# RWKV-7 recurrence in chunks: level 0 of the triangular inverse taken from the left sides by copies and 32x32 transposes

## The reference, cut to what matters

```python
def step(S, inp):
    r_t, w_t, k_t, v_t, kk_t, a_t = inp
    sa = jnp.einsum('bhvk,bhk->bhv', S, kk_t)
    S = S * w_t[:, :, None, :] - sa[..., None] * (kk_t * a_t)[:, :, None, :] + v_t[..., None] * k_t[:, :, None, :]
    y = jnp.einsum('bhvk,bhk->bhv', S, r_t)
    return S, y
S, ys = lax.scan(step, S0, xs)
```

## Time and profile before

| what | value |
|---|---|
| median of 3 runs | 1197.93 us (1197.78 to 1203.37) |
| the profiled execution | span 1197.4 us; the page gives no other time of it |
| four units of the recurrence | 411 to 611 us |
| their successor: last steps, output projection, routing, experts | 611 to 1197 us |
| TensorE busy | 1120.7 us (94%) |
| VectorE, ScalarE, GpSimd busy | 464.6, 363.2, 259.6 us |
| mean granted TensorE clock | 0.980 |

### The profile page before, as it was taken

How to read it: one execution, slowest core, us unless ns; L and a number is a source line. 1 busy time by engine, 2 the same in 40 slices (tenths; PEclk the granted TensorE clock), 3 DMA queues, 4 the chain that set the end, 5 groups by cost and what they waited for, 6 DMA issues and landing times.

```text
span 1197.4 us, 24875 instructions
## 1 busy us (share of the span) xinstructions
PE 1120.7 (94%) x10856; PEld 785.9 (66%) x10856; DVE 464.6 (39%) x930; ACT 363.2 (30%) x808; POOL 259.6 (22%) x153
## 2 busy tenths in 40 slices
PE   5999999999999988788889999889999999999995
PEld 4666666655566667667654444478778887888774
DVE  4200657447765586675835422441101000111034
ACT  3101545444334365563621311111111111011152
POOL 0000000001110179999800000111112112111102
PEclk9999999999999999999999999889999999999998
DMA  6511100010010210002051661268889989998894
GB/s 207 153 36 36 57 18 19 18 31 27 25 37 18 35 37 4 5 4 56 7 182 36 236 226 71 93 221 306 268 310 323 312 290 319 322 322 295 299 387 170
DMA packets 95689, 174.16 MB, mean 145 GB/s; under 512 B 19988, under 2 KB 41175, under 8 KB 95172
## 3 DMA queue, kind: packets, MB, share of 16 engines
q1 hardware_dynamic: 88372, 151.92, 36.6%
q0 software_dynamic: 7200, 20.57, 6.4%
HBM read 147.45 MB, written 27.75 MB: 146 GB/s over the span
## 4 chain that ended last, share of the span: by engine, by line
PE 85%; DVE 8%; ACT 3%; issue 3%; SPq 0%; DMA 0%; POOLq 0%; POOL 0%; DVEq 0%; ACTq 0%
PE ps L740 23%; PE ps L1446 20%; PE ps L1244 9%; PE ps L1469 9%; PE ps L1475 1%; PE ps L819 1%; PE ps L843 1%; PE ps L832 1%; PE ps L1422 1%; PE ps L956 1%; PE ps L944 1%; PE ps L997 1%; PE ps L1099 1%; PE ps L1122 1%; PE ps L1309 1%
## 5 line engine op out<-in xcount | busy, mean ns | idle before, releaser
L740 PE MATMUL ps<-arena 128*128 128x355 f32 x960 | 299.3, 468 | 2.2 <-issue 2.1
L1446 PEld LDWEIGHTS ps<-arena 128*128 128x128 f32 x2048 | 245.9, 191 | 7.8 <-issue 6.1
L740 PEld LDWEIGHTS ps<-arena 128*128 128x128 f32 x960 | 180.2, 191 | 107.6 <-issue 10.4
L1446 PE MATMUL ps<-arena 128*128 128x128 f32 (+4 forms) x2048 | 248.3, 283 | 0.7 <-ACT arena L1958 0.6
L1244 PE MATMUL ps<-arena 128*128 128x512 f32 x256 | 116.6, 597 | 0.9 <-DVE arena L2346 0.7
L1469 PE MATMUL ps<-arena 128*128 128x512 f32 x256 | 113.3, 595 | 0.7 <-DVE arena L2621 0.7
L1966 ACT ACTIVATE arena<-ps 128x128 f32<-128x128 f32 (+4 forms) x64 | 18.3, 286 | 278.5 <-PE ps L1446 278.5
L2621 DVE TENSOR_TENSOR arena<-arena,ps 128x128 f32<-128x128 f32 (+4 forms) x64 | 19.1, 299 | 212.7 <-ACT arena L1966 212.7
L1469 PEld LDWEIGHTS ps<-arena 128*128 128x128 f32 x256 | 47.4, 190 | 55.1 <-issue 53.6
L2806 POOL TENSOR_TENSOR arena<-arena 128x1024 f32<-128x1024 f32 x4 | 11.4, 2858 | 330.5 <-DVE arena L2147 330.5
L1555 ACT COPY arena<-ps 128x355 f32<-128x355 f32 x60 | 27.2, 453 | 183.1 <-PE ps L740 183.1
(11 more groups left out here) (416 smaller groups left out, 1567.4 us busy)
## 6 DMA issues: line engine op xcount, KB each, us to landing
arena<-in_w_exp_gate SPq DMA_DIRECT2D x16, 2048.0 KB
arena<-in_w_exp_up SPq DMA_DIRECT2D x16, 2048.0 KB
arena<-in_w_exp_down SPq DMA_DIRECT2D x16, 2048.0 KB, 15.4
arena<-in_w_in SPq DMA_DIRECT2D x16, 512.0 KB, 3.8
arena<-in_x_prompt SPq DMA_DIRECT2D x9, 512.0 KB, 4.5
x_dram<-arena SPq DMA_DIRECT2D x9, 512.0 KB, 3.6
h_dram<-arena SPq DMA_DIRECT2D x8, 512.0 KB, 2.6
out_y_prompt<-arena SPq DMA_DIRECT2D x8, 512.0 KB, 3.5
```

The costliest lines, as they stand in the source:

```text
L740: last = pe.matmul(ps[:, q % 2, 0:m], wr[:, n % 3, k, :], hT[:, k, a:a + m], start=(k == 0), stop=(k == KB - 1))
L1446: last = pe.matmul(ps[:, 3 + f % 2, n * CAP:n * CAP + CAPS[e]], w[a][:, k, f * P:(f + 1) * P], xgT[:, a, k, 0:CAPS[e]], start=(k == 0), st ...
```

## The change

Level 0 is no longer computed by products of its own. The identities go into U (not TL); a predicated copy puts the level-0 entries of the raw left side (B side, from PSUM) into U, under the transposed level mask. ScalarE copies U to TT (64 partitions at a time where rows are exchanged), VectorE turns U by 32x32 blocks into TL. ScalarE, not VectorE, copies the B side out, both banks in one copy and without a mask. The mask of its second half follows at the end of the unit (`r_reaching`), and `r_ra` waits for it. TensorE's order becomes `r_left` 0, 1, `r_u(0, 1)`, `r_gain` 0, `r_u(1, 1)`, `early_fill`, `r_gain` 1, `step`, `r_x(0, 1)`.

```diff
@@ TensorE
-            def r_cross(hp, b):                 (its 32 products per unit go)
             def r_gain(hp, b):
-                pe.wait_ge(s["rl_ok"], 4 * m + 4)
+                pe.wait_ge(s["rl_ok"], 4 * hp + b + 3)
             def r_u(hp, b, lv):
                 if lv == 1:
-                    pe.wait_ge(s["rc_ok"], m + 1)
+                    pe.wait_ge(s["rl_act"], m + 1)
+                    pe.wait_ge(s["tr_own"], nth(hp, b, 1, LV - 1))
             def r_ra(hp, b):
                 pe.wait_ge(s["rm_ok"], 2 * m + 2)
+                pe.wait_ge(s["lm_ok"], m + 1)
-                r_cross(hp, 0)
-                r_gain(hp, 0)
                 for lv in range(1, LV):
                     r_u(hp, 0, lv)
                     if lv == 1:
-                        r_cross(hp, 1)
+                        r_gain(hp, 0)
+                        r_u(hp, 1, lv)
+                        early_fill(hp, lv)
                         r_gain(hp, 1)
-                        early_fill(hp, lv)
-                        r_u(hp, 1, lv)
                         step(hp, c)
@@ ScalarE
+            def left_raw(hp, b):
+                act.wait_ge(s["rl_ok"], 4 * hp + b + 1)
+                act.copy(LB[:, b].rearrange("p u j c -> p u (j c)"), ps[:, 4 * b:4 * b + 2, :]).then_inc(s["rl_act"], 1)
+            def first_turned(hp, b):
+                act.wait_ge(s["rl_ok"], 4 * hp + b + 1)
+                flat = lambda ap: ap.rearrange("p j t -> p (j t)")
+                for e in range(2):
+                    act.copy(flat(TT[row(e), b, JB:2 * JB, :]), flat(U[row(1 - e), b, JB:2 * JB, :]))
+                act.copy(flat(TT[:, b, 0:JB, :]), flat(U[:, b, 0:JB, :])).then_inc(s["tr_ok"], 1)
             def u_out(hp, b, lv):
+                if lv == 1:
+                    act.wait_ge(s["tr_ok"], nth(hp, b, 1, LV - 1))
-                    act.copy(TL[:, b], T["eye64"]...).then_inc(s["r_eye"], 1)
+                    act.copy(U[:, b], T["eye64"]...).then_inc(s["r_eye"], 1)
-                gained(hp, 0)
+                left_raw(hp, 0)
+                first_turned(hp, 0)
+                left_raw(hp, 1)
                 for lv in range(1, LV):
-                    swap_rows(hp, 0, lv - 1)
+                    if lv > 1:
+                        swap_rows(hp, 0, lv - 1)
                     u_out(hp, 0, lv)
+                    if lv == 1:
+                        first_turned(hp, 1)
+                        gained(hp, 0)
                     first_fill(hp, lv)
+                    if lv > 1:
+                        swap_rows(hp, 1, lv - 1)
+                    u_out(hp, 1, lv)
                     if lv == 1:
                         gained(hp, 1)
                         if hp >= 2:
                             sf_copy(hp - 2, 3)
-                    swap_rows(hp, 1, lv - 1)
-                    u_out(hp, 1, lv)
@@ VectorE
+            def r_paired(hp, b):
+                dve.wait_ge(s["r_eye"], m + 1)
+                dve.wait_ge(s["rl_ps"], 2 * m + 1)
+                src = ps[:, 4 * b:4 * b + 2, :].rearrange("p u (j c) -> p u j c", j=JB)[:, :, :, 0:CH]
+                dve.copy_predicated(U[:, b]..., lm(0, 1, 2 * JB)..., src).then_inc(s["rl_ok"], 1)
+            def r_first(hp, b):
+                dve.wait_ge(s["rl_ok"], 4 * hp + b + 1)
+                for u in range(2):
+                    hs = slice(JB * u, JB * (u + 1))
+                    last = dve.transpose(TL[:, b, hs, :]..., U[:, b, hs, :]...)
+                last.then_inc(s["tr_own"], 1)
+            def r_masked(hp, b):                (K side alone, one signal for two multiplies)
+            def r_reaching(hp, b):
+                dve.wait_ge(s["rl_act"], m + 1)
+                x = LB[:, b, :, :, CH:]
+                dve.tensor_tensor(x, x, T["m64"][:, None, None, CH:].to_broadcast([P, 2, JB, CH]), ALU.mult).then_inc(s["lm_ok"], 1)
-                r_masked(hp, 0, 0)
-                r_masked(hp, 0, 1)
-                r_crossed(hp, 0)
-                r_masked(hp, 1, 0)
-                r_transpose(hp, 0, 0)
-                r_masked(hp, 1, 1)
-                r_crossed(hp, 1)
+                r_paired(hp, 0)
+                r_first(hp, 0)
+                r_paired(hp, 1)
+                r_first(hp, 1)
+                r_masked(hp, 0)
+                r_masked(hp, 1)
                 for lv in range(1, LV):
-                    r_transpose(hp, 1, lv - 1)
+                    if lv > 1:
+                        r_transpose(hp, 1, lv - 1)
                 ...
                 if hp >= 2:
                     g_scale(hp - 2, 1, 3)
+                for b in range(NB_):
+                    r_reaching(hp, b)
+                if hp >= 2:
                     g_final(hp - 2, 1, 3)
```

More of the change, by code:

```diff
@@ L73 @@
 kvs_ok bias_in level_ok sc_ps sc_ok m_ok e_ok p_norm pt_ps pt_ok ob_ps ob_ok gamma_ok
[L74 removed]
+rt_ps rt_act rt_dve r_eye rl_ps rl_act rl_ok lm_ok rg_ps rg_ok ru_ps ru_ok rx_ps rx_ok rxt_ps rxt_ok rm_ps rm_ok
 rra_ps re_ok rs_ps rs_ok ryl_ps ryl_ok rsc_ps rsb_ok ryy_ps ry_ok sf_ps sf_ok
@@ L958, in r_left @@
                     last.then_inc(s["rl_ps"], 1)
-            def r_cross(hp, b):
-                m = 2 * hp + b
-                pe.wait_ge(s["rl_ok"], 4 * m + 2)
-                for j in range(JB):
-                    for e, u in QUAD:
-                        ct = chunk(2 * (JB * b + j) + e)
-                        last = pe.matmul(ps[row(e), 4 * b + u, j * CH:(j + 1) * CH], z_of(hp)[row(u), ct], NBT[hp][row(u), ct], start=True, stop=True)
-                last.then_inc(s["rc_ps"], 1)
             def r_gain(hp, b):
                 m = 2 * hp + b
-                pe.wait_ge(s["rl_ok"], 4 * m + 4)
+                pe.wait_ge(s["rl_ok"], 4 * hp + b + 3)
                 for j in range(JB):
@@ L1819, in _ @@
                         act.wait_ge(s["mixed"], 14)
-                    act.copy(TL[:, b], T["eye64"][:, None, :].to_broadcast([P, 2 * JB, CH])).then_inc(s["r_eye"], 1)
+                    act.copy(U[:, b], T["eye64"][:, None, :].to_broadcast([P, 2 * JB, CH])).then_inc(s["r_eye"], 1)
                 if hp == 1:
                     b_square(2)
-                gained(hp, 0)
+                left_raw(hp, 0)
+                first_turned(hp, 0)
+                left_raw(hp, 1)
                 for lv in range(1, LV):
-                    swap_rows(hp, 0, lv - 1)
+                    if lv > 1:
+                        swap_rows(hp, 0, lv - 1)
                     u_out(hp, 0, lv)
+                    if lv == 1:
+                        first_turned(hp, 1)
+                        gained(hp, 0)
                     first_fill(hp, lv)
+                    if lv > 1:
+                        swap_rows(hp, 1, lv - 1)
+                    u_out(hp, 1, lv)
                     if lv == 1:
@@ L2252, in r_turned, with r_masked @@
                 dve.tensor_copy(ZG[row(0), b, 1, :, 0:HD], zt[row(1), :, 1]).then_inc(s["rt_dve"], 1)
-            def r_masked(hp, b, n):
+            def r_paired(hp, b):
                 m = 2 * hp + b
-                if m == 0 and n == 0:
-                    dve.wait_ge(s["scaled"], 2 * HP)
-                dve.wait_ge(s["rl_ps"], 2 * m + n + 1)
-                for u in range(2):
-                    src = ps[:, 4 * b + 2 * n + u, :].rearrange("p (j c) -> p j c", j=JB)
-                    dve.tensor_tensor((LB, LK)[n][:, b, u], src, m64, ALU.mult).then_inc(s["rl_ok"], 1)
-            def r_crossed(hp, b):
-                dve.wait_ge(s["r_eye"], 2 * hp + b + 1)
-                dve.wait_ge(s["rc_ps"], 2 * hp + b + 1)
-                for u in range(2):
-                    last = dve.copy_predicated(TL[:, b, JB * u:JB * (u + 1), :], lm(0, 0, JB), ps[:, 4 * b + u, 0:JB * CH].rearrange("p (j c) -> p j c", j=JB))
-                last.then_inc(s["rc_ok"], 1)
+                dve.wait_ge(s["r_eye"], m + 1)
+                dve.wait_ge(s["rl_ps"], 2 * m + 1)
+                src = ps[:, 4 * b:4 * b + 2, :].rearrange("p u (j c) -> p u j c", j=JB)[:, :, :, 0:CH]
+                dve.copy_predicated(U[:, b].rearrange("p (u j) t -> p u j t", u=2), lm(0, 1, 2 * JB).rearrange("p (u j) t -> p u j t", u=2), src).then_inc(s["rl_ok"], 1)
+            def r_first(hp, b):
+                dve.wait_ge(s["rl_ok"], 4 * hp + b + 1)
+                for u in range(2):
+                    hs = slice(JB * u, JB * (u + 1))
+                    last = dve.transpose(TL[:, b, hs, :].rearrange("p j t -> p (j t)"), U[:, b, hs, :].rearrange("p j t -> p (j t)"))
+                last.then_inc(s["tr_own"], 1)
+            def r_masked(hp, b):
+                dve.wait_ge(s["rl_ps"], 2 * (2 * hp + b) + 2)
+                for u in range(2):
+                    src = ps[:, 4 * b + 2 + u, :].rearrange("p (j c) -> p j c", j=JB)
+                    last = dve.tensor_tensor(LK[:, b, u], src, m64, ALU.mult)
+                last.then_inc(s["rl_ok"], 1)
+            def r_reaching(hp, b):
+                m = 2 * hp + b
```

(11 more changed lines are left out.)

3 lines of the change are left out of this document (1 added, 2 removed).

## The result

The changed kernel takes 1210.82 us (median of 4 runs, 1206.91 to 1213.53) against 1197.86 for the kernel before: a ratio of 1.0103, 95% interval 1.0072 to 1.0134. In a second set of runs it stood at 1.0061 (1.0036 to 1.0086). It is slower; 1192.7 was forecast, and slower by over 0.5% had a chance of 0.04. The profiled execution of the changed kernel took 1210.47 us, its span is 1208.3. Of the 10.9 us between the two profiled spans 3.7 lie ahead of the first L956, in code that the change does not touch, and 7.6 in the recurrence.

What follows compares the result with a forecast made beforehand. VectorE's queue was taken to set each head's end, by way of `gained`, in a chain across three engines. Gains of 2.6 + 0.6 + 1.0 + 1.15 less 0.1 made 5.25 us off, giving 1192.7 us; range 1188.5 to 1198.5.

Steps and rivals of the forecast that it cites:

- What the heads would do: Start of each unit, from L956: a step-by-step timeline with shorter heads, 9.2 to 9.3 us in units 2 and 3.
- The late mask: `r_reaching` on VectorE at the unit's end: two masks of 0.68 us, nearly covered, costed at 0.1 us in all.
- the bound of 3.6 us for a pair: Late masks beside GpSimd: 1.8 us each, from GpSimd's 4.53 us for 2048 columns, 1.13 for 512.
- the collision as a rival: Late masks meet GpSimd's work on SBUF: 3.0 us lost, 1195.7 us; chance 0.07, shared with the filler's case.
- The cover in unit 0: Unit 0's late masks were to run in the time in which ScalarE copies M.
- The sum of the heads: Gains of 2.6, 0.6, 1.0 and 1.15 us in units 0 to 3, less 0.1 for late masks: 5.25 us.
- Level 1 and the steps follow from there in a fixed pattern: Behind `gained` in each unit: a head ending earlier should move the program's end by as much.
- Outside the heads nothing is added: Rest of the kernel: no added time; `r_ra`'s new wait for the late masks counted as met, 0.1 us in all.
- The clock rival: Half-clock spells in the units, at most about 1.7 us each: two fewer 1189.3 us (chance 0.20), two more 1196.1 (0.13).

Runs made afterwards that it cites:

- the two kernels that take the mask elsewhere: Changed kernel with the late masks taken out of PSUM by VectorE in the head (ratio 1.0024), or issued by GpSimd between its own instructions (1.0015).
- both loads moved: Output weight's load put behind the sample recurrence, sample state's load held past unit 0's level 2 products: kernel before 1.0146, changed kernel with masks on GpSimd 1.0208.
- the products issued twice: Changed kernel with the late masks on GpSimd, and level 1's 32 `r_u` matmuls of each half issued twice: 1200.56 us, ratio 1.0009.
- the mask from PSUM: Changed kernel, but ScalarE copies the strict half alone and VectorE masks the other half out of PSUM in the head: 1201.28 us, ratio 1.0024.
- only the state's load held back: Sample state's load alone held until unit 0 has copied its level 2 products: ratio 1.0101 with masks on GpSimd, 1.0015 with masks from PSUM, 1.0031 for kernel before.
- the mask on GpSimd: Changed kernel with the eight late masks issued by GpSimd between its instructions of the sample recurrence: 1201.42 us, ratio 1.0015.
- one mask per unit: Changed kernel with the two late masks of a unit made one VectorE instruction of 1024 columns: 1203.04 us, ratio 1.0018.

## Why the prediction was wrong

*What the heads would do.* Right: x of half 0 at 9.52, 10.85, 9.47 and 9.46 us (forecast 9.7, 10.7, 9.15, 9.15), `left_raw` 1.01 (1.03), the turned copies 0.82 + 0.41 (1.14), the filler of unit 3 waiting for `gained` 0 and `r_gain` 1 behind it. The 0.3 us in units 2 and 3 are not ScalarE's: its 64x256 copies took 0.40 each, not 0.366, but `gained` 0 ended 7.49 us after L956 in unit 3, forecast 7.54. They came behind it, in the hand-overs of the chain that follows: `r_gain` 1 at 7.84 (forecast 7.72), `gained` 1 at 8.60 (8.42), the first step at 9.33 (9.06).

*The step that failed* is "**The late mask** ... I cost it at 0.1 us in all", with the bound of 3.6 us for a pair. The pair took up to 9.17. I had the collision as a rival, but priced it as a slower rate, GpSimd's 4.53 us for 2048 columns divided by four. The bound to take was the length of the GpSimd instruction, 4.54 us, once for each mask: two waits and two own times, up to 10.4 us for a pair. The rival had the place wrong as well: it put 2.3 us on unit 2, 0.7 on unit 1 and nothing on unit 0, where TensorE stood 4.8 us, against 6.0 in unit 1. The cover in unit 0 was there for a pair at its own rate: TensorE had work until 451.06, 2.6 us after the first mask began. By the two kernels that take the mask elsewhere it costs 0.4 to 0.9% of the time (1.0061 and 1.0103 against 1.0015 and 1.0024), 4 to 11 us; added to the kernel before, 0.72%. The timeline of before showed GpSimd's instructions one behind the other from 426 to 594, so any position in units 0 to 2 was beside one.

*The sum of the heads*, 5.25 us, came true at the points that it was made for, and in part by luck. At level 2's first x in unit 0 and at x of half 1 in the others the first two profiles differ by 2.67, 1.07, 1.56 and 0.79 us, 6.1 in all, but two of the heads of before had met half clock and none of the changed ones did. The kernel before with both loads moved shows three of its heads at full clock, with the changed one's beside them; the first fence is the kernel before, the second the changed head, each with both loads late:

```profile
414.62:425.99 11.37, 7.69 (x321) 6.82 (x325) 10.48 (x21) 3.64 (x8) 1.09 (x1) 1.00 0.34 40
460.97:471.38 10.41, 8.27 (x325) 7.04 (x328) 8.24 (x18) 5.49 (x11) 10.22 (x3) 1.00 0.02 3
509.51:519.33 9.82, 7.69 (x327) 7.03 (x327) 7.66 (x17) 4.43 (x10) 9.66 (x3) 1.00 0.02 3
```

```profile
414.66:424.19 9.53, 6.11 (x256) 5.62 (x260) 8.79 (x17) 6.35 (x13) 1.09 (x1) 1.00 0.31 43
457.49:468.34 10.85, 7.41 (x264) 6.11 (x264) 5.93 (x12) 9.03 (x17) 10.61 (x4) 1.00 0.02 4
506.44:515.90 9.46, 6.39 (x262) 5.92 (x262) 5.93 (x12) 8.32 (x17) 9.23 (x4) 1.00 0.01 3
```

Unit 1's head is 0.44 us longer, not 0.6 shorter, and unit 2's gain is 0.36. At the points of the sum the kernel before with both loads late stands at 16.18, 12.39, 11.95 and 11.94 us after L956, the changed one at 13.54, 12.74, 11.35 and 11.35: at full clock 3.5 us are gained, 2.6 of them in unit 0, as forecast there.

"Level 1 and the steps follow from there in a fixed pattern" held in unit 3, the one unit that ran at full clock in both first profiles as far as `r_ra`: 0.79 us gained at x of half 1, 0.80 at the transposed product `r_xt` and 0.80 at `r_ra`. "Outside the heads nothing is added" failed behind that point: from L956 to `r_read` unit 3 took 75.31 us before and 75.27 after.

*What takes it back*, besides the mask, is the term that the sum did not have, TensorE's wait for its own instructions. Of the 0.76 us given back in unit 3 behind `r_ra`, 0.66 lie in such gaps: one of 0.77 us before, of 0.94 and 0.50 after. In the whole recurrence these gaps hold 7.2 us before, and 10.7 to 13.0 in the three kernels with the changed head and no mask late on VectorE (9.2 with the products issued twice). The gaps, the clock and the head can't be added up to the microsecond, as a wait in one place covers part of another. The Trainium skill (Runtime: NRT & Kernel Launch, "Instruction fetch mechanics") has each engine fetch its instructions by a DMA queue of its own and calls the cost mostly hidden. The trace agrees on the queue and not on the cost: beside a full load the gap was 4.4 us, and without any load beside it up to 1.9 us.

*The clock rival* was sized at two spells either way. The kernel before had 6.8 us missing in the units, the changed one 8.6 and 22.2 in two profiles. The five profiles without a late wait on VectorE and with the loads in their place have 3.4 to 6.8, the six with it 8.6 to 22.2: that speaks for counting low clock to the price of the mask. It is not the mask's alone: the mask from PSUM and the kernel before, each with only the state's load held back, have 10.2 without a late mask, and in the kernel with the mask on GpSimd the granted clock stood at 0.50 right behind both of its gaps of 4.4 us (from 430.8 and from 560.5). How much the mask adds is not settled, as the two profiles of one kernel differ by 13.6.

No version beat the kernel before. Five are level with it (the mask from PSUM, and that with the state's load late; the mask on GpSimd, and that with the products twice; one mask per unit), at 1.0009 to 1.0024 with 1 inside every interval; the mask from PSUM is the simplest.

## What to carry to other kernels

Before a VectorE instruction goes into idle time, look at what GpSimd does there: with two operands in SBUF, or one at the fast rate, it can cost the whole GpSimd instruction that is running, for each VectorE instruction anew. Read such an operand from PSUM, merge two instructions into one, or give the work to GpSimd itself. Compare a forecast stretch with a stretch of before at the same clock, and follow it to the end of the unit. And where an engine works through many short instructions, look for gaps without a releaser and set them beside the packets of its instruction queue: a chain made shorter was worth here only what the supply of instructions let through.

## What the runs showed that I had not expected

A 128x512 multiplication by a constant, fp32 in SBUF, took 0.42 us alone and up to 4.72 us beside GpSimd's 128x2048 instructions; copies out of PSUM, masks out of PSUM with a table from SBUF, predicated copies and transposes beside the same instructions took their usual time. GpSimd loses by it too, but little: its 3.62 us instruction took 3.94, its 4.54 us ones 4.88 and 4.82. A load that fills the DMA engines (share about 1, 1 to 1.5 MB) went with up to 5.5 us in which TensorE did nothing (3.1 to 4.7 in unit 2 in most profiles), at the place in its stream that fell there, whatever the product was; TensorE went on 1.2 to 1.7 us after the 16 KB packet with its instructions had landed.
